# A two-layer decoder trunk on one core: gate and up products of the experts from high and low parts

## The reference

```python
D_MODEL = 1024; N_GROUPS = 4; EXPERTS_PER_GROUP = 8; TOP_K = 2; D_EXPERT = D_MODEL // 4
...
def hierarchical_moe(h, w_group, b_group, w_router, b_router, w_gate, w_up, w_down):
    ...
    def expert_block(args):
        xb, e = args
        return (jax.nn.silu(xb @ w_gate[e]) * (xb @ w_up[e])) @ w_down[e]
    ...
    y = jax.ops.segment_sum(y_buf[dest] * sw[:, None].astype(y_buf.dtype), st, num_segments=T)
```

## Time and profile before

| | |
|---|---|
| median of 3 runs | 3559.33 us (3557.93 to 3562.45) |
| the profiled execution | 3558.93 us, its span 3557.1 us |
| granted TensorE clock, mean | 0.949 |
| busy share of the span: PE, DVE, ACT, POOL | 90%, 50%, 35%, 50% |
| DMA | 535.63 MB, mean 151 GB/s |
| first and last transposes of experts | 894.5 and 3384.3 us |

### The profile page before, as it was taken

One profiled execution on the slowest core, in us unless ns is written; L12 is line 12 of the kernel. 1 busy time (PEld: TensorE's weight loads), 2 busy tenths in 40 slices (PEclk: granted clock), 3 DMA queues, 4 the chain that ended last, 5 costly groups with the idle time before them and its releaser, 6 DMA issues. The chain is left out here.

```text
span 3557.1 us, 57727 instructions
## 1 busy us (share of the span) xinstructions
PE 3198.7 (90%) x20065; PEld 2492.4 (70%) x20065; DVE 1765.5 (50%) x3672; ACT 1249.4 (35%) x2673; POOL 1791.8 (50%) x1443
## 2 busy tenths in 40 slices
PE   6999998997999995997999999999998987999950
PEld 4788886785888884996566666666656876888840
DVE  3555555676343333664554554555534663433316
ACT  2444444232223222443443444444343222232212
POOL 2555554343344431444689778877872223444312
PEclk9999999998999997998899999999999998999975
DMA  2010102642999975886320221021005439999817
GB/s 100 26 39 26 39 33 74 194 153 92 369 317 306 304 244 171 254 266 173 67 51 7 51 54 48 10 51 51 7 13 188 145 113 318 360 313 312 292 66 325
DMA packets 357633, 535.63 MB, mean 151 GB/s; under 512 B 81873, under 2 KB 277749, under 8 KB 350532
## 3 DMA queue, kind: packets, MB, share of 16 engines
q1 hardware_dynamic: 330468, 456.94, 40.1%
q0 software_dynamic: 26976, 76.27, 5.6%
HBM read 396.93 MB, written 144.92 MB: 152 GB/s over the span
## 5 line engine op out<-in xcount | busy, mean ns | idle before, releaser
L2074 POOL TENSOR_TENSOR ab_acc<-ab_acc,ab_pT 128x1024 f32<-128x1024 f32 (+2 forms) x320 | 593.5, 1855 | 129.0 <-ACT ab_pT L2108 96.4
L2108 ACT ACTIVATE ab_pT<-ab_S 128x512 f32<-128x512 f32 (+4 forms) x704 | 352.5, 504 | 560.3 <-PE ab_S L2185 301.2
L2124 DVE TENSOR_REDUCE ab_mx<-ab_W 128x2 f32<-128x1024 f32 (+5 forms) x352 | 346.4, 994 | 377.7 <-PE ab_W L2200 252.1
L1264 POOL DMA_INDIRECT scratch_y<-ex_y,ex_prow x64 | 64.8, 1012 | 491.9 <-issue 353.0
L1434 PE MATMUL ex_G<-ex_xT,ex_wg 128*128 128x160 f32 x2048 | 293.3, 302 | 2.7 <-DMA ex_wu<-in_moe_w_up 2.7
L1434 PE MATMUL ex_U<-ex_xT,ex_wu 128*128 128x160 f32 x2048 | 288.6, 299 | 0.0
L2183 PE MATMUL ab_S<-ab_q_hi,ab_k_hi 97*128 97x512 f32 (+4 forms) x704 | 279.6, 397 | 9.5 <-ACT ab_pT L2108 8.3
L1434 PEld LDWEIGHTS ex_G<-ex_xT,ex_wg 128*128 128x128 f32 x2048 | 281.6, 191 | 7.8 <-issue 3.6
L2234 PE MATMUL ab_O<-ab_pT,ab_v 128*64 128x512 f32 (+4 forms) x1408 | 283.9, 519 | 0.0
L1434 PEld LDWEIGHTS ex_U<-ex_xT,ex_wu 128*128 128x128 f32 x2048 | 281.7, 190 | 0.0
L2184 PE MATMUL ab_S<-ab_q_lo,ab_k_hi 96*128 96x512 f32 (+4 forms) x704 | 249.9, 355 | 0.0
(11 more groups left out here) (308 smaller groups left out, 7041.4 us busy)
## 6 DMA issues: line engine op xcount, KB each, us to landing
ex_wg<-in_moe_w_gate SPq DMA_DIRECT2D x64, 1024.0 KB, 7.0
ex_wu<-in_moe_w_up SPq DMA_DIRECT2D x64, 1024.0 KB, 10.7
ex_wd<-in_moe_w_down SPq DMA_DIRECT2D x64, 1024.0 KB, 11.8
pb_y<-scratch_y SPq DMA_DIRECT2D x17, 1024.0 KB, 6.8
pr_o<-scratch_oT SPq DMA_DIRECT2D x33, 512.0 KB, 4.7
scratch_h<-pr_h SPq DMA_DIRECT2D x33, 512.0 KB, 5.0
scratch_xn<-pr_xn SPq DMA_DIRECT2D x33, 512.0 KB, 2.7
fi_y<-scratch_y SPq DMA_DIRECT2D x16, 1024.0 KB, 14.0
```

The costliest lines, as they stand in the source:

```text
L2074: nc.gpsimd.tensor_tensor(to, to, pT[0:r, U % RING, :, 0:n], ALU.add).then_inc(added, 1)
L2108: nc.scalar.activation(pT[0:r, U % RING, h, 0:n], S[0:r, h, 0:n], ACT.Exp, scale=B_SCALE).then_inc(exped, 1)
L2124: nc.vector.reduce_max(mx[:, :, t, c:c + 1].rearrange("p h a -> p (h a)"), W[:, j % 2, :, 0:n], AX.X).then_inc(emptied, 1)
```

## The change

- Gate and up products are made from parts. `wg_hi`, `wg_lo`, `wu_hi`, `wu_lo` are single buffers. The transposed tokens `xT` hold the high parts in columns 0 to 159 and the low ones in 160 to 319, so one product with the high weights has 320 columns and one with the low weights 160; DVE adds the two halves (`reduce_sum` into `gsum`, `usum`).
- ACT makes the high parts of tokens, gate and up weights, each in two pieces; DVE the low parts.
- The low part of the down weights moves from DVE to GpSimd (`lower_down`), and its high part from ACT's step for g to the end of the step for f.
- Gate and up weights come as contiguous 8 KB for each partition instead of 1 KB pieces, so partition p holds rows 8p to 8p + 7 of a weight. For that the normed tokens `xn` are written permuted by DVE (a strided write), and the router's weights and the transposes of `experts_beyond` follow.
- `wg`, `wu`, `x`, `xr` are two deep instead of four.
- TensorE makes the gate products between the transposes of `x` and those of the rest.

```diff
-                        nc.vector.scalar_tensor_tensor(out=xn[:, j.slot, :], in0=h[:, j.slot, :], scalar=rstd[:, j.slot:j.slot + 1],
-                                                       in1=gain[:, :], op0=ALU.mult, op1=ALU.mult).then_inc(xn_ready, 1)
+                        nc.vector.scalar_tensor_tensor(out=xn[:, j.slot, :].rearrange("p (c q) -> p q c", c=DC),
+                                                       in0=h[:, j.slot, :].rearrange("p (q c) -> p q c", c=DC), scalar=rstd[:, j.slot:j.slot + 1],
+                                                       in1=gain[:, :].rearrange("p (q c) -> p q c", c=DC), op0=ALU.mult, op1=ALU.mult).then_inc(xn_ready, 1)
...
+        wg = s.sb("wg", [P, 2, DC, FE])
+        wu = s.sb("wu", [P, 2, DC, FE])
+        wg_hi, wg_lo = s.sb("wg_hi", [P, DC, FE], F32R), s.sb("wg_lo", [P, DC, FE], F32R)
+        wu_hi, wu_lo = s.sb("wu_hi", [P, DC, FE], F32R), s.sb("wu_lo", [P, DC, FE], F32R)
...
+        x = s.sb("x", [P, 2, D])
+        xr = s.sb("xr", [P, 2, QD4])
+        xT = s.sb("xT", [P, 2, DC, 2 * CAP], F32R)
+        gsum = s.sb("gsum", [P, FC, CAP])
+        usum = s.sb("usum", [P, FC, CAP])
...
+                        if e.after(2):
+                            sp.wait_ge(g_split, e.back(2).count(2, 2))
+                        sp.dma_start(wg[:, e.slot, :, :].rearrange("p c f -> p (c f)"),
+                                     pick(io["moe_w_gate"][layer].rearrange("e (p c) f -> e p (c f)", c=DC), e)).then_inc(g_in[e.slot], 16)
+                        if e.after(2):
+                            sp.wait_ge(u_split, e.back(2).count(2, 2))
+                        sp.dma_start(wu[:, e.slot, :, :].rearrange("p c f -> p (c f)"),
+                                     pick(io["moe_w_up"][layer].rearrange("e (p c) f -> e p (c f)", c=DC), e)).then_inc(u_in[e.slot], 16)
...
+                    if e.after(2):
+                        pool.wait_ge(flipped, e.back(2).count(3, 3))
...
+                def lower_down(f):
+                    pool.wait_ge(d_high, f.count(1, 1))
+                    nc.gpsimd.tensor_tensor(wd_lo[:, :, :].rearrange("p c f -> p (c f)"), wd[:, f.slot4, :, :].rearrange("p c f -> p (c f)"),
+                                            wd_hi[:, :, :].rearrange("p c f -> p (c f)").bitcast(F32), ALU.subtract).then_inc(d_split, 1)
...
+                    if e.back(1).live(EXPERTS):
+                        lower_down(e.back(1))
                     f = e.back(2)
                     if f.live(EXPERTS):
                         pool.wait_ge(y_act, f.count(2, 2))
...
+                def raise_weights(e, high, raw, arrived, used, done):
+                    act.wait_ge(arrived[e.slot], (e.uses + 1) * 16)
+                    if e.after(1):
+                        act.wait_ge(used, e.count(1, 0))
+                    for b in range(2):
+                        nc.scalar.copy(high[:, 4 * b:4 * b + 4, :].rearrange("p c f -> p (c f)"),
+                                       raw[:, e.slot, 4 * b:4 * b + 4, :].rearrange("p c f -> p (c f)")).then_inc(done, 1)
...
+                        raise_x(e, 0)
+                        raise_x(e, 1)
+                        raise_weights(e, wg_hi, wg, g_in, gated, g_high)
+                        raise_rest(e)
                     if f.live(EXPERTS):
...
+                        act.wait_ge(g_summed, f.count(1, 1))
+                        nc.scalar.activation(gsum[:, :, :].rearrange("p c t -> p (c t)"), gsum[:, :, :].rearrange("p c t -> p (c t)"), ACT.Silu).then_inc(silued, 1)
+                    if e.live(EXPERTS):
+                        raise_weights(e, wu_hi, wu, u_in, upped, u_high)
                     if g.live(EXPERTS):
                         if g.after(2):
                             act.wait_ge(y_out[g.slot], g.uses * 32)
...
                         nc.scalar.copy(y[:, g.slot, 0:512], Y[:, g.c % 2, :]).then_inc(y_act, 1)
                         act.wait_ge(downed, g.count(3, 3))
                         nc.scalar.copy(yr[:, g.slot, :], Y[:, g.c % 2, 0:QD4]).then_inc(y_act, 1)
+                    if f.live(EXPERTS):
+                        act.wait_ge(d_in[f.slot4], (f.uses4 + 1) * 16)
+                        if f.after(1):
+                            act.wait_ge(downed, f.back(1).count(3, 3))
+                        nc.scalar.copy(wd_hi[:, :, :].rearrange("p c f -> p (c f)"), wd[:, f.slot4, :, :].rearrange("p c f -> p (c f)")).then_inc(d_high, 1)
...
+                def lower_x(e, b):
+                    dve.wait_ge(x_high, e.count(3, 1 + b))
+                    low_part(xT[:, e.slot, 4 * b:4 * b + 4, CAP:CAP + P], T[:, (b + e.c) % 2, :].rearrange("p (c t) -> p c t", t=P),
+                             xT[:, e.slot, 4 * b:4 * b + 4, 0:P]).then_inc(x_split, 1)
...
+                def lower_weights(e, low, high, raw, raised, done):
+                    for b in range(2):
+                        dve.wait_ge(raised, e.count(2, 1 + b))
+                        low_part(low[:, 4 * b:4 * b + 4, :].rearrange("p c f -> p (c f)"), raw[:, e.slot, 4 * b:4 * b + 4, :].rearrange("p c f -> p (c f)"),
+                                 high[:, 4 * b:4 * b + 4, :].rearrange("p c f -> p (c f)")).then_inc(done, 1)
+
...
                     if e.live(EXPERTS):
-                        dve.wait_ge(flipped, e.count(3, 2))
...
+                        lower_x(e, 0)
+                        lower_x(e, 1)
+                    if f.live(EXPERTS):
+                        dve.wait_ge(gated, f.count(1, 1))
+                        nc.vector.reduce_sum(gsum[:, :, :], G[:, :, 0:2 * CAP].rearrange("p k (a t) -> p k t a", a=2), AX.X).then_inc(g_summed, 1)
+                    if e.live(EXPERTS):
+                        lower_weights(e, wg_lo, wg_hi, wg, g_high, g_split)
+                        lower_rest(e)
                     if e.back(-1).live(EXPERTS):
                         find_places(e.back(-1))
-                    if e.turn is None and 1 <= e.c <= 10:
-                        list_beyond(e.c)
                     if f.live(EXPERTS):
+                        dve.wait_ge(upped, f.count(1, 1))
+                        nc.vector.reduce_sum(usum[:, :, :], U[:, :, 0:2 * CAP].rearrange("p k (a t) -> p k t a", a=2), AX.X).then_inc(u_summed, 1)
+                        dve.drain()
                         if f.after(2):
                             dve.wait_ge(downed, f.back(2).count(3, 3))
                         dve.wait_ge(silued, f.count(1, 1))
-                        nc.vector.tensor_tensor(h[:, f.slot, :, :].rearrange("p c t -> p (c t)"), act_g[:, f.slot, :, :].rearrange("p c t -> p (c t)"),
-                                                U[:, f.slot, 0:FC * CAP], ALU.mult)
+                        nc.vector.tensor_tensor(h[:, f.slot, :, :].rearrange("p c t -> p (c t)"), gsum[:, :, :].rearrange("p c t -> p (c t)"),
+                                                usum[:, :, :].rearrange("p c t -> p (c t)"), ALU.mult)
                         dve.drain()
                         nc.vector.tensor_copy(h_hi[:, f.slot, :, :], h[:, f.slot, :, 0:P])
                         dve.drain()
                         low_part(h_lo[:, f.slot, :, :], h[:, f.slot, :, 0:P], h_hi[:, f.slot, :, :]).then_inc(h_ready, 1)
+                    if e.live(EXPERTS):
+                        lower_weights(e, wu_lo, wu_hi, wu, u_high, u_split)
+                    if e.turn is None and 1 <= e.c <= 10:
+                        list_beyond(e.c)
                     if g.live(EXPERTS):
                         if g.after(2):
                             dve.wait_ge(y_out[g.slot], g.uses * 32)
...
+                def gate(f, out, high, low, split, freed, done):
+                    pe.wait_ge(split, f.count(2, 2))
+                    if f.after(1):
+                        pe.wait_ge(freed, f.count(1, 0))
+                    for k in range(FC):
+                        for c in range(DC):
+                            nc.tensor.matmul(out[:, k, 0:2 * CAP], high[:, c, P * k:P * k + P], xT[:, f.slot, c, :], start=(c == 0), stop=False)
+                            last = nc.tensor.matmul(out[:, k, 0:CAP], low[:, c, P * k:P * k + P], xT[:, f.slot, c, 0:CAP], start=False, stop=(c == DC - 1))
+                    last.then_inc(done, 1)
+
...
+                            if e.after(1):
+                                pe.wait_ge(x_split, e.back(1).count(3, 2 + b))
...
+                    if f.live(EXPERTS):
+                        pe.wait_ge(x_split, f.count(3, 3))
+                        gate(f, G, wg_hi, wg_lo, g_split, g_summed, gated)
+                    if e.live(EXPERTS):
+                        pe.wait_ge(x_split, e.count(3, 1))
+                        pe.wait_ge(xr_in[e.slot], (e.uses + 1) * 16)
...
                     if f.live(EXPERTS):
-                        pe.wait_ge(gu_in[f.slot4], (f.uses4 + 1) * 32)
...
-                        for w, out in ((wg, G), (wu, U)):
-                            for k in range(FC):
```

(5 more changed lines are left out.)

99 lines of the change are left out of this document (37 added, 62 removed).

## The result

The changed kernel takes **3838.36 us** (median of 4 runs, 3836.84 to 3839.99) against 3560.01 (4 runs, 3557.93 to 3562.45): ratio 1.0783, 95% interval 1.0771 to 1.0796. Forecast was +179 us, measured is +278. The profiled executions span 3836.5 and 3557.1 us.

The account below looks back on a forecast made before the run. TensorE bounds the kernel before; afterwards a two-round path through GpSimd, landing, DVE and the lock gives 16.8 us rounds. 3558.9 + 168 (64 experts) + 11 (stage ends) = 3738 us, range 3515 to 3865.

Parts of the forecast that it names:

- TensorE's part: Gate and up products at 0.15 us per wide and 0.115 per narrow pass; TensorE alone needs 13.83 us an expert.
- GpSimd's price: Low part of the down weights, 2048 elements, costs 4.58 us on GpSimd, twice what DVE needed.
- Landing: Time L from a scatter's issue to its landing, taken as 6 us, with ends 2.2 and 7.2.
- The closed path through TensorE: From down products through ACT, GpSimd, scatter landing, DVE and back to TensorE: 24.2 + L us over two rounds.
- Rounds that miss and rounds that are hit will alternate: Lock on GpSimd's next low part hits or misses (misses from a 16.1 us round); middle 16.8 us, +168 us.
- 17.4: Round in us if GpSimd's next 4.58 us hold up's low part on the path: (30.2 + 4.58)/2.
- rival 3: Lock hits every round and TensorE's clock falls: rounds 18.6 to 19.8 us, 3850 to 3930 us; chance 0.13.
- The lock: GpSimd's 4.58 us shut out DVE instructions with two SBUF inputs, catching at least up's low part: +4.58 on the path.
- The token write at 0: Strided write of xn: 40 us at most if it doubled, taken as 0 because TensorE has work there.
- The stage ends: At both stages' ends TensorE waits 2.3 us longer for down's low part; first gate products start 3.3 later: +11 us.
- Pieces of 8 KB and two-deep buffers at 0: Larger weight pieces spare DMA time nothing waits for; shallower buffers are refilled early enough: 0 us.
- Rival 1: Faster, TensorE stays the bound because the scatter lands in 3.7 us or less: 13.83 us rounds, 3537 us; chance 0.17.

Follow-up runs that it names:

- experiment 2: Changed kernel, but DVE again makes the down weights' low part, behind the tokens' low parts; GpSimd keeps only gathers and scatters: 3644.35 us, ratio 1.0233.
- experiment 6: Two tries on the changed kernel: GpSimd's low part in four instructions, 3819.51 us; 28 unread transposes added on TensorE ahead of the rest transposes, 3889.08 us.
- experiment 1: Changed kernel with DVE making the next expert's places at the end of its round, behind y: 3544.38 us, ratio 0.9945 to the kernel before.
- experiment 5: Changed kernel with both scatters ahead of GpSimd's low part and DVE's places last: 3703.88 us, ratio 1.0398.
- experiment 7: Layout alone in the kernel before: 3571.36 us, ratio 1.0032; further runs turned the token write round or moved the extra-block list, lowest 3516.90 us.

## Why the prediction was right, and where its size was wrong

- **TensorE's part: right in sum, for wrong reasons.** A pair of passes takes 0.26 us (1101.61 to 1101.84 and on), 0.265 was forecast. But the wide pass takes 0.18 and not 0.15, the narrow one 0.075 and not 0.115: a narrow pass has no floor of 0.11 here. TensorE's round is 13.25, not 13.83. Of the 0.58 us between them 0.12 is in the products (8.36 for 8.48), 0.38 in the transposes, which run in 0.99 us where they had 1.61 with a wait of 0.24, and 0.08 in the down products.
- **GpSimd's price: right.** 4.62 and 4.55, median 4.59, against 4.58.
- **Landing: right.** 5.4 us behind GpSimd's low part, 7.4 in the other rounds, 6 taken.
- **The closed path through TensorE: right, term by term to within 0.6 us, but for one.** From 1100.76 to 1137.56 it measures: down's high part 2.40, low part and hop 4.77, scatters 2.14, landing 5.46, places 0.39, sum 0.99, h with the lock 5.37, low part of up 2.27, y 0.60, sources 0.49, tokens 0.74, rest transposes 0.34, up products 6.93, down products 3.91. That is 36.8 for two rounds; I had 24.2 + 6 + 4.58 = 34.8. The term off is the up products, 6.93 for 4.24.
- **The step that failed** is the last one: "Rounds that miss and rounds that are hit will alternate, and I take the middle, 16.8". It took both rounds of a pair as equally long, with GpSimd's next low part at 17.55 us of the path. That part came at 15.83 (1116.59 behind 1100.76), because TensorE doesn't wait in the round between, which is 13.25 however long the pair gets; so it falls on h in nearly every pair, and the length of 16.1 from which it should miss doesn't come into it. 17.4 already counts one hit in two rounds and followed from my own sum. And the wait of a pair doesn't spread over its rounds but comes in one piece, mostly of 7 to 8.7 us, behind which TensorE runs at 1.2 GHz: I had tied the clock to rival 3, "hit in every round", and it needs only one hit in two. The up products lost 26.5 us to it in 26 rounds, 1.0 each; 17.4 and 1.0 are 18.4, and 18.25 was measured (26 rounds from 949.99 to 1424.57). The two expert stages grew by 258.9 us where 168 and 11 were forecast: 80 of the 100 us missing. The other 21 are in the token writes.
- **A path that I didn't see:** y, scatters, landing, places, y, one round long. In experiment 2 it set the time. In the changed kernel it stands some 3 us behind the one that I had (33.5 and 36.8 for two rounds), so the sum came out near without it; that is luck, and the expectations of experiments 2 and 6, which were 109 and 149 us short, showed the gap.
- **The lock: right in mechanism and size,** shown in both directions by experiments 1 and 5, which differ in GpSimd's order alone. That it falls on h was not forecast; I had it on up's low part.
- **The token write at 0: wrong.** "TensorE has work there" doesn't hold for the last tile before a transposition waits. It is +11 us by experiment 7 (21 in the profiles of the changed kernel).
- **The stage ends** came out at 6.86 us of waiting instead of 4.62, 2.24 more as forecast (read at the first stage's end); the first gate product is only 0.6 to 0.9 us later behind the first transposes, not 3.3. Pieces of 8 KB and two-deep buffers at 0: right.
- **Rival 1** was a kernel one edit away: without the wait for the places the round is 13.25.

## What to carry to other kernels

A wait in the middle of an engine's order costs what is queued behind it: before asking what a new piece of work costs, look for waits that are harmless only because nothing urgent stands behind them, and move those to the end of the step first. Follow every closed path, also those that leave out the bound engine, since one that is a little shorter takes over as soon as the longest is repaired, and ask of each step on it what ended its wait: a path whose steps wait for something outside it isn't the one that sets the time. A helper engine that shares a lock is nearly free or costs 160 us (the two stages took 933 before) depending on which instruction it lands beside, so choose its place by the operands of its neighbours.

## What I had not expected of the hardware

- An fp32r pass of 160 columns follows the one ahead in 0.075 us at 2.4 GHz, though it loads new 128x128 weights (191 ns in the record, beside other passes); passes of 144 columns in another stage stood 0.11 apart.
- Behind 7.17 us of standstill the first 6 us or so of passes ran at half the clock, 1.2 GHz (pairs 0.48 us apart, 0.26 later). The length of the wait alone doesn't tell it: the up products took 4.18 us behind a wait of 2.39 us (experiment 2, round from 1285.18) and 5.76 behind one of 1.69 (round from 1163.96).
- GpSimd's instruction that issues a scatter is held by DVE too: 2.52 us instead of 0.99 when it meets DVE's low part of down (1171.30 to 1173.58), though it computes nothing. The forecast had this for a gather only the earlier trace rows.
- A fp32 write on DVE with a stride of 512 bytes costs 0.6 of its time more (1.34 to 2.13 us), reads of two inputs with 32 bytes still more (2.39).
